# The begin of a decoder-layer kernel: smaller first transfers split at once, an activation table loaded ahead, and matmuls of zeros before the data

## The reference, cut to what matters

```python
def rmsnorm(x, g):
    xf = x.astype(jnp.float32)
    y = xf * lax.rsqrt(jnp.mean(xf * xf, axis=-1, keepdims=True) + EPS)
    return (y * g.astype(jnp.float32)).astype(x.dtype)
...
        h = rmsnorm(x, g_mix[l])
        (nq, nkc, nvc, nks, nvs, nkw, nvw, ngt, mq, mk, mv, mo, mi, mf) = split_cols(h @ w_in[l], IN_SIZES)
```

## Time and profile before

| what | value |
|---|---|
| median of 3 runs | 1656.57 us (1655.55 to 1657.11) |
| span of the profiled execution, first to last instruction | 1653.0 us |
| PE busy | 1617.6 us, 98% of the span |
| DVE busy | 1204.2 us, 73% |
| ACT busy | 725.1 us, 44% |
| POOL busy | 873.2 us, 53% |
| chain that ended last, share of PE | 61% |

### The profile page before, as it was taken

How to read it: one execution, slowest core, us unless ns; L and a number is a source line. 1 busy time by engine, 2 the same in 40 slices (tenths; PEclk the granted TensorE clock), 3 DMA queues, 4 the chain that set the end, 5 groups by cost and what they waited for, 6 DMA issues and landing times.

```text
span 1653.0 us, 22437 instructions
## 1 busy us (share of the span) xinstructions
PE 1617.6 (98%) x8126; PEld 1346.8 (81%) x8126; DVE 1204.2 (73%) x1599; ACT 725.1 (44%) x1389; POOL 873.2 (53%) x676
## 2 busy tenths in 40 slices
PE   7998999999999999999999999999999999999997
PEld 6887888887888888898888878778888888887886
DVE  6765888887788875464555457788887887888955
ACT  5114888885322342253233134344444444533444
POOL 3233555454333334303226343599988878789841
PEclk9999999999999999999999999999999999999999
DMA  5130201110111132242100431345434444874522
GB/s 195 60 131 27 65 27 39 37 42 27 52 64 39 50 117 102 101 154 90 39 26 28 151 115 38 131 166 178 175 134 141 140 145 167 304 282 140 167 82 102
DMA packets 80426, 176.46 MB, mean 107 GB/s; under 512 B 7932, under 2 KB 24508, under 8 KB 80192
## 3 DMA queue, kind: packets, MB, share of 16 engines
q1 hardware_dynamic: 68040, 135.71, 24.1%
q10 hardware_dynamic: 12280, 39.34, 6.3%
HBM read 136.21 MB, written 38.81 MB: 106 GB/s over the span
## 4 chain that ended last, share of the span: by engine, by line
PE 61%; DVE 17%; POOL 10%; ACT 6%; issue 6%; DMA 1%; ACTq 0%; POOLq 0%; DVEq 0%; SPq 0%
PE ps L1104 14%; PE ps L1108 14%; PE ps L1107 14%; DVE x_t L3036 4%; PE ps L1305 4%; POOL sum_s L1015 3%; ACT x_t L2219 2%; PE ps L1327 2%; POOL w_lo L1009 2%; PE ps L1328 2%; DVE x_t L3065 2%; POOL s_new L1035 1%; DVE ps L3028 1%; ACT w_hi L2206 1%; PE ps L1268 1%
## 5 line engine op out<-in xcount | busy, mean ns | idle before, releaser
L1104 PE MATMUL ps<-h_hi,w_hi 128*128 128x512 f32 x1060 | 418.3, 395 | 3.9 <-ACT p_sum L2188 2.3
L1108 PE MATMUL ps<-h_hi,w_lo 128*128 128x512 f32 x1060 | 413.0, 390 | 0.0
L1107 PE MATMUL ps<-h_lo,w_hi 128*128 128x512 f32 x1060 | 412.9, 390 | 0.0
L913 POOL TENSOR_TENSOR w_hi<-w_raw,ones 128x1024 fp32r<-128x1024 f32 x51 | 103.3, 2025 | 493.8 <-PE ps L1104 471.7
L1104 PEld LDWEIGHTS ps<-h_hi,w_hi 128*128 128x128 f32 x1060 | 199.0, 188 | 52.5 <-ACT p_sum L2188 8.7
L1108 PEld LDWEIGHTS ps<-h_hi,w_lo 128*128 128x128 f32 x1060 | 199.0, 188 | 42.3
L1107 PEld LDWEIGHTS ps<-h_lo,w_hi 128*128 128x128 f32 x1060 | 199.2, 188 | 38.5
L952 POOL TENSOR_SCALAR probs<-probs,nsa_inv,gate_sig 128x640 f32<-128x640 f32 (+7 forms) x128 | 100.8, 788 | 128.5 <-DVE nsa_inv L2608 128.3
L3036 DVE SCALAR_TENSOR_TENSOR x_t<-ps,par,x_t 128x1023 f32<-128x1023 f32 x84 | 107.7, 1282 | 72.7 <-ACT x_t L2219 71.2
L918 POOL TENSOR_TENSOR w_lo<-w_raw,w_hi 128x1024 fp32r<-128x1024 f32 x51 | 136.5, 2676 | 3.9
L2391 DVE TENSOR_TENSOR pt_lo<-ps,pt_hi 128x512 fp32r<-128x512 f32 (+6 forms) x148 | 100.4, 683 | 11.9 <-ACT pt_hi L1903 10.2
(11 more groups left out here) (415 smaller groups left out, 4027.1 us busy)
## 6 DMA issues: line engine op xcount, KB each, us to landing
w_raw<-in_w_tiles SPq DMA_DIRECT2D x109, 512.0 KB, 3.3
w_raw<-in_w_tiles SPq DMA_DIRECT2D x55, 256.0 KB, 3.2
s_new<-in_w_tiles SPq DMA_DIRECT2D x44, 256.0 KB, 4.0
z_dram<-x_t ACTq DMA_DIRECT2D x21, 512.0 KB, 2.9
b<-z_dram SPq DMA_DIRECT2D x33, 256.0 KB, 3.6
q_st<-q_dram SPq DMA_DIRECT2D x64, 128.0 KB, 2.9
x_dram<-x_t ACTq DMA_DIRECT2D x14, 512.0 KB, 2.8
t_dram<-t_new ACTq DMA_DIRECT2D x22, 256.0 KB, 5.1
```

What stands on the lines that cost most here:

```text
L913: pool.tensor_tensor(w_hi[s][:, :], w_raw[s][:, :], ones[:, :].to_broadcast([P, KT * P]), ALU.mult).then_inc(w_hi_made.sem, w_hi_made.up())
L1104: ins = mm(out_ap, whi, x_hi, start=first, stop=False)
L1107: mm(out_ap, whi, x_lo, start=False, stop=False)
L1108: return mm(out_ap, wlo, x_hi, start=False, stop=last)
```

## The change

It touches the begin, and two small things at the end.

- **SP's loads.** The two weight tiles come in two pieces each: the first 256 columns (`BEGUN = 2` blocks of 128; 128 KB) and the other 768 (384 KB). The order is now: parameters, first piece of tile 0, first piece of tile 1, x block 1, rest of tile 0, rest of tile 1, x blocks 2 to 7, then as before. x block 0 is no longer SP's: ACT issues it in two halves (256 KB each) on its own queue, before anything else it does.
- **ACT.** After these two DMAs it waits for a tile of zeros and runs one copy of a column of it (`junk`), which makes the activation table load come there. Then: high part of the first piece of tile 0, the wait for the parameters, the high part of x block 0 in two halves, the first piece of tile 1, x block 1, rest of tile 0, x block 2, rest of tile 1; then it alternates square k, high part of block k+3 (k+2 before).
- **DVE.** It sets the zeros first, then goes on as before, with the low parts in ACT's new order and the loop as low part of block k+3, add of square k.
- **PE.** It waits for the zeros, runs three float32 matmuls of zeros (512, 512 and 256 columns) into a bank that is unused then, and starts the products without waiting for the masks, for which it now waits before `token_sums`. Step 0 waits for x block 0 half by half; step `BEGUN` waits for the rest of each weight tile.
- **POOL** waits for one more count (nine low parts instead of eight).
- **The end.** One semaphore counts all output stores; the final gain is counted on `gains_loaded`.

```diff
         @block.sync
-            def load_first(z):
-                sp.dma_start(wf_raw[z][:, :], w_tiles[z, :, :]).then_inc(t(f"wf_loaded{z}", 16).sem, 16)
+            def load_first(z, rest):
+                cs = slice(BEGUN * P, KT * P) if rest else slice(0, BEGUN * P)
+                told = t(f"wf_loaded{z}" if rest else f"wf_begun{z}", 16)
+                sp.dma_start(wf_raw[z][:, cs], w_tiles[z, :, cs]).then_inc(told.sem, 16)
...
-            load_first(0)
-            load_x(0)
+            load_first(0, False)
+            load_first(1, False)
             load_x(1)
-            load_first(1)
+            load_first(0, True)
+            load_first(1, True)
             for k in range(2, KT):
                 load_x(k)
...
         @block.gpsimd
             x_split = t("x_split")
-            x_split.add(KT)
+            x_split.add(KT + 1)
             pool.wait_ge(x_split.sem, x_split.value())
...
         @block.tensor
-            masks_ready.add(3)
-            pe.wait_ge(masks_ready.sem, masks_ready.value())
+            pe.wait_ge(t("zeros_made").sem, 1)
+            for n in (HALF, HALF, HALF // 2):
+                mm(ps[:, 7, 0:n], zeros[:, 0:P], zeros[:, 0:n], start=True, stop=True)
...
             for k in range(KT):
                 pe.wait_ge(x_split.sem, x_split.next())
                 for z in range(FIRST):
-                    if k == 0:
+                    if k == 0 or k == BEGUN:
                         pe.wait_ge(piece_split.sem, piece_split.next())
                     w = (wf_hi[z][:, k * P:k * P + P], wf_lo[z][:, k * P:k * P + P])
                     for c in range(2):
+                        if k == z == 0 and c:
+                            pe.wait_ge(x_split.sem, x_split.next())
...
+            masks_ready.add(3)
+            pe.wait_ge(masks_ready.sem, masks_ready.value())
             token_sums(acc_x, 6)
...
         @block.scalar
-            gains_loaded = t("gains_loaded", 16)
-            gains_loaded.add(1)
-            act.wait_ge(gains_loaded.sem, gains_loaded.value())
+            for c, told in ((0, t("block_loaded0", 16)), (1, t("x_half_loaded", 16))):
+                cs = slice(c * HALF, c * HALF + HALF)
+                act.dma_start(x_f[:, 0, cs], x_rows[0, :, cs]).then_inc(told.sem, 16)
+            act.wait_ge(t("zeros_made").sem, 1)
+            f(junk[:, :], zeros[:, 0:1], ACT.Copy).then_inc(junk_written.sem, junk_written.up())
...
-            first_high(0)
-            x_high(0)
+            first_high(0, False)
+            gains_loaded = t("gains_loaded", 16)
+            gains_loaded.add(1)
+            act.wait_ge(gains_loaded.sem, gains_loaded.value())
+            x_high_half(0)
+            x_high_half(1)
+            first_high(1, False)
             x_high(1)
-            first_high(1)
+            first_high(0, True)
+            x_high(2)
+            first_high(1, True)
             for k in range(KT):
                 x_square(k)
-                if k + 2 < KT:
-                    x_high(k + 2)
+                if k + 3 < KT:
+                    x_high(k + 3)
...
         @block.vector
+            dve.memset(zeros[:, :], 0.0).then_inc(t("zeros_made").sem, 1)
             clear_sums(acc_x)
...
-            first_low(0)
-            x_low(0)
+            first_low(0, False)
+            x_low(0, slice(0, HALF))
+            x_low(0, slice(HALF, SEQ))
+            first_low(1, False)
             x_low(1)
-            first_low(1)
+            first_low(0, True)
+            x_low(2)
+            first_low(1, True)
             for k in range(KT):
-                if k + 2 < KT:
-                    x_low(k + 2)
+                if k + 3 < KT:
+                    x_low(k + 3)
                 add_square(k % 2, acc_x, sq_x)
```

More of the change, by code:

```diff
@@ L43 @@
 FIRST = 2
+BEGUN = 2
 FIRST_KV = 11 - FIRST + 4 * MH + KT
@@ L384, in build @@
         acc_x = at("acc_x", FREE + 64 * KB, [P, SEQ])
+        zeros = at("zeros", FREE + 68 * KB, [P, HALF])
+        junk = at("junk", FREE + 70 * KB, [P, 1])
         r_in = at("r_in", FREE + 72 * KB, [P, SEQ])
@@ L854, in _ @@
                     sp.wait_ge(conv_done.sem, conv_done.value())
-                    sp.dma_start(gain_bc[:, :], final_gain[:, :]).then_inc(t("gain_loaded", 16).sem, 16)
-            stored = [t(f"stored{b}", 16) for b in range(4)]
+                    sp.dma_start(gain_bc[:, :], final_gain[:, :]).then_inc(t("gains_loaded", 16).sem, 16)
+            stored = t("stored", 16)
             for i in range(4, TT):
@@ L1552, in _ @@
             out_slot, piece_split = [], t("piece_split")
-            piece_split.n = FIRST
+            piece_split.n = 2 * FIRST
             def first_outputs(z, c, k0, k1):
@@ L1780, in column_root, with first_high, x_high_half @@
                     std_ready.sem, std_ready.up())
-            gains_loaded = t("gains_loaded", 16)
-            gains_loaded.add(1)
-            act.wait_ge(gains_loaded.sem, gains_loaded.value())
-            def first_high(z):
-                act.wait_ge(t(f"wf_loaded{z}", 16).sem, t(f"wf_loaded{z}", 16).next())
-                f(wf_hi[z][:, :], wf_raw[z][:, :], ACT.Copy).then_inc(t("piece_high").sem, t("piece_high").up())
+            for c, told in ((0, t("block_loaded0", 16)), (1, t("x_half_loaded", 16))):
[3 more added lines that the diff above has]
+            f(junk[:, :], zeros[:, 0:1], ACT.Copy).then_inc(junk_written.sem, junk_written.up())
+            def first_high(z, rest):
+                cs = slice(BEGUN * P, KT * P) if rest else slice(0, BEGUN * P)
+                told = t(f"wf_loaded{z}" if rest else f"wf_begun{z}", 16)
+                act.wait_ge(told.sem, told.next())
+                f(wf_hi[z][:, cs], wf_raw[z][:, cs], ACT.Copy).then_inc(t("piece_high").sem, t("piece_high").up())
+            def x_high_half(c):
+                told, cs = (t("block_loaded0", 16), t("x_half_loaded", 16))[c], slice(c * HALF, c * HALF + HALF)
+                act.wait_ge(told.sem, told.next())
+                f(h_hi[:, 0, cs], x_f[:, 0, cs], ACT.Copy, scale=gains[:, G_MIX, 0:1]).then_inc(hi_ready.sem, hi_ready.up())
             def x_high(k):
@@ L2428, in _, with first_low, x_low @@
             dve.wait_ge(t("gains_loaded", 16).sem, t("gains_loaded", 16).value())
-            def first_low(z):
+            def first_low(z, rest):
+                cs = slice(BEGUN * P, KT * P) if rest else slice(0, BEGUN * P)
                 dve.wait_ge(t("piece_high").sem, t("piece_high").next())
-                low(wf_lo[z][:, :], wf_raw[z][:, :], wf_hi[z][:, :]).then_inc(t("piece_split").sem, t("piece_split").up())
-            def x_low(k):
+                low(wf_lo[z][:, cs], wf_raw[z][:, cs], wf_hi[z][:, cs]).then_inc(t("piece_split").sem, t("piece_split").up())
+            def x_low(k, cs=slice(0, SEQ)):
                 wait_hi()
-                low(h_lo[:, k, :], x_f[:, k, :], h_hi[:, k, :], gains[:, G_MIX, k:k + 1]).then_inc(
+                low(h_lo[:, k, cs], x_f[:, k, cs], h_hi[:, k, cs], gains[:, G_MIX, k:k + 1]).then_inc(
                     x_split.sem, x_split.up())
-            first_low(0)
-            x_low(0)
+            first_low(0, False)
+            x_low(0, slice(0, HALF))
+            x_low(0, slice(HALF, SEQ))
+            first_low(1, False)
             x_low(1)
-            first_low(1)
+            first_low(0, True)
+            x_low(2)
+            first_low(1, True)
             for k in range(KT):
-                if k + 2 < KT:
-                    x_low(k + 2)
+                if k + 3 < KT:
+                    x_low(k + 3)
                 add_square(k % 2, acc_x, sq_x)
@@ L3166, in _ @@
                 down_step(g)
-            dve.wait_ge(t("gain_loaded", 16).sem, 16)
+            t("gains_loaded", 16).add(1)
+            dve.wait_ge(t("gains_loaded", 16).sem, t("gains_loaded", 16).value())
             def finish_tokens(i, src):
```

15 lines of the change are left out of this document (7 added, 8 removed).

## The result

The median of the changed kernel is **1659.74 us** (1657.08 to 1661.13, 17 runs), that of the kernel before, run beside it on the same chip, 1655.89 us (1655.21 to 1657.54, 17 runs). The ratio is 1.0022, with a 95% interval from 1.0016 to 1.0029: slower by 3.85 us. The forecast was 1656.1, and the range ended at 1659.4, so the median lies 0.3 us outside it, on its slow side. The profiled execution took 1657.38 us with a span of 1655.6; 1.7 to 1.8 us lie outside the span, in it as in every other profiled execution here. One execution of before in its repeat ran at a granted clock of 0.56 and took 2705 us; it is left out of every number.

What follows compares the result with a forecast made beforehand. PE was 98% busy, but DVE's adds of squares gated token_sums, limiting what a faster begin could win. Sums at 34.2 against 34.66 shift -0.45 us: 1656.57 - 0.45 = 1656.1 us, range 1653.2 to 1659.4.

Steps and rivals of the forecast that it cites:

- who is next in line: At token_sums, DVE's adds of squares come next after PE; a faster begin alone wins 1.46 us.
- nothing shows that it must fall in this one: PE's new 4.2 us wait before token_sums: the argument against a clock fall there, the trace having one such fall only.
- B: Rival at PE's new wait: clock falls, stretch behind the sums runs cold, up to 2.95 lost, +2.5 us, 1659.1; chance 0.33.
- A: Forecast case at token_sums: DVE's adds take PE's place, the clock holds, -0.45 us; chance 0.55 together with D.
- D: Rival at the begin: table load or zeros fail, PE's 4.2 us wait absorbs it, still -0.45 us; 0.55 with A.
- shift of -0.45: At token_sums: block 2 lands at 11.16, four adds end at 34.11, sums start at 34.2 against 34.66.
- bound of +0.7: Shift at token_sums if block 2 lands at 12.3, through another loss from smaller packets or two queues.
- First product: PE's start: first product at about 5.6 us (between 5 and 6.5) against 10.06.
- Zeros: PE's start: products of zeros run from 1.6 to 5.9 us and raise the clock before about 8 rather than 15.9.
- table load: ACT's start: 1.28 us moved beside the first transfers, worth 1.28 us to the first product, contained in the 5.6.
- Other edits: POOL's count, masks wait, store semaphore and final gain's name: no waiting order changes, worth nothing.
- C: Rival at token_sums: adds done by 30 do not bind, 4.6 us won, 1652.0; chance 0.12 including mixtures with early landings.

Runs made afterwards that it cites:

- the two variants with a wait of 3.6 and 4.1 us: Changed kernel without its three products of zeros: 1659.35 us, 1.0019; changed kernel with x block 0 issued on SP's queue: 1661.00 us, 1.0027.

## Why the prediction was wrong, point by point

- **The structure held.** The four adds were forecast at 8.54 us from 25.57, and took 8.71 from 25.74; the last product over near 30.0, and it was at 31.4; a wait near 4.2 us, and it is 3.2, 4.1 and 2.5 us in three profiles. PE's last product was over 2.1 to 4.0 us earlier than in the profile of before, and the wait took all of it: that is the forecast's reading of who is next in line, and it was right.
- **The step that failed: "nothing shows that it must fall in this one".** B had a chance of 0.33 and A with D 0.55. The clock fell in or behind this wait in three of three profiles of after, and in the two variants with a wait of 3.6 and 4.1 us; filled, the same wait let it fall in none of five. The row on which B rested, a fall some 3 us behind the last matmul, was a measurement of the very quantity in question, and the forecast wait was longer. "The trace has one such fall only" spoke for the lack of other long waits, not against B. The Trainium skill's rule that was quoted (TensorE: Matmul & The Clock Gate, HAM oscillation) pointed to B, and the traces bear it out.
- **B's term was mis-sized.** It was put at "up to 2.95", the price of the begin. It is 1.6, 4.3 and 1.7: the sums can run cold too, and the stretch can last 10 us (33.6 to 43.8). B with -0.45 gave +2.5 at most; the mean of 2.5 and a shift of +0.4 give +2.9, and +4.3 was reachable.
- **The shift of -0.45 was not there.** In the first profile block 2's high part starts at 11.30, as landed at about 11.2 for a forecast 11.16, and block 3's low part at 15.21 for 15.06, so this profile is right to 0.4 us at the sums (34.60 for 34.2). In the other two the high part starts at 11.56 and 11.80, and the sums follow at 34.83 and 35.11. But a forecast was set against one execution of before, 34.66, which was the latest of its three. On the means the sums come 0.4 us later. The bound of +0.7, for a loss "from smaller packets or two queues", held it; the value taken did not. The rate of 271 GB/s (261 to 279 in the kernels with these loads) against 310 to 328 goes with such a loss; the second queue is not its cause, and the smaller pieces were not tried alone.
- **First product: 5.6 forecast, 7.76 measured**, 1.3 outside of the step's own bounds. The transfers were the mis-sized term: ACT waits for the first piece until 5.89, where 3.6 to 5 was the forecast for piece and block together. It cost nothing, since the wait would have absorbed it. With block 0 on SP's queue the first product came at 6.31 and 6.71.

```profile
1.75 1.28 ACT L1797 ACT_TABLE_LOAD   x1 [1.75 <-PEq L3248]
...
5.89 0.42 ACT L1803 ACTIVATE wf_hi<-wf_raw 128x256 fp32r<-128x256 f32 x1 [2.64 <-DMA wf_raw<-in_w_tiles]
```

- **Zeros: worth nothing, as forecast, and less sure than forecast.** They end at 5.9, as forecast, and taking them out changes nothing. They were to bring the clock up before 8 us: in two profiles of after the first products are warm (7.76 and 7.20), in the third they are cold up to 13.8. **The table load** sits at 1.75, beside the first transfers; it was not tried alone.
- **Other edits: nothing, as forecast.** The shift of the last matmuls is 2.7 us and the spans differ by 2.6, so the end costs nothing.
- **C: did not happen**, and the two kernels with POOL kept away show what it would take: sums at 31.2 to 31.9.
- **Span and median.** The 3.6 us between them were taken as one fixed difference. 1.7 to 1.8 are; the rest was that this profile was the fastest of before's three (1653.0, 1654.4, 1654.8), without the cold stretch at 130 us. It did no harm to the sum, but it hid a term of 1.6 us that comes and goes, in the kernel from which all was read.

What is accounted for: of the 3.0 us between the mean spans, 0.4 by the later sums and 2.5 by the clock behind them. The cold stretch at 130 us, in three of three profiles of after and two of three of before, adds 0.5, of which 0.3 are back by 200 us. The medians of all runs are 3.85 apart; the last 0.8 is not settled, since no typical execution of after was profiled. A price of 3.3 us, as in the two variants with a cold stretch of 6.8, would cover it; that is argued, not shown.

## What to carry to other kernels

Before a begin is made faster, find what must also be there when the faster engine arrives (here the adds on DVE, slowed by POOL beside them); the gain beyond it becomes a wait, and a wait of TensorE of 2.2 to 4.1 us is not free, since it cost 1.6 to 4.3 us of clock behind it. Take away the cause of the wait (POOL's start, and work shared with ACT) rather than fill it with empty products: that gave 4.7 to 5.2 us against after, the fill 1.2. Even so the clock fell in one of three profiles with a wait of no more than 0.6 us, and nothing was won against the kernel before that is clear of noise. And read the same stretch in more than one profile of the kernel before a difference of half a microsecond is worked out from it.

## What the runs showed of the hardware

- Matmuls of one column, or transposes of 4 to 24 columns, do not reliably keep the clock up: in the first profile of after PE is busy for 97% of the time from 123 to 128 us and the clock falls all the same (0.68 in the stage from 128 to 129, 0.50 in the next); after a wait of 2.50 us and 1.9 us of sums it fell too (37.8), and once after a wait of 0.59 and 1.92 us of sums (34.8). The first profile of before did not fall near 128 us.
- Products of zeros can bring the clock up and can hold it: with the first at 1.53, the 512-column matmuls at 7.8 to 8.8 us are 0.23 apart, at full clock; then 8.9 to 12.3 is cold, behind the wait of 1.88 us ahead of 7.76. Without zeros they are cold from 7.2 to 11.2. In another profile with the same zeros they are cold from 7.7 to 13.8. So the zeros at the start won little; those in the wait held the clock in five profiles of five.
- DVE's add of 128x1024 takes 1.22 us alone, and 2.7 and 3.2 beside POOL's operations on a tile of the same size, of which the first goes from 1.9 to 2.8. Four adds: 5.20 and 8.71 us.
- PEclk prints 1.00 ahead of the first change of the clock, also where the matmuls are 0.43 us apart, so in the begin only the distance of the starts tells.
